# Expert stage in plain fp32 on groups of 32 array columns, raw weights in a ring of 18 pieces

## The reference

```python
logits = (t @ w_router).astype(jnp.float32)          # t: 256 x 1024
top_v, top_i = lax.top_k(logits, TOP_K)              # TOP_K = 2 of 8 experts
top_p = jax.nn.softmax(top_v, axis=-1)
combine = jnp.sum(jax.nn.one_hot(top_i, N_EXPERTS) * top_p[..., None], axis=1)
for e in range(N_EXPERTS):
    out = out + combine[:, e:e + 1] * swiglu(t, w_gate[e], w_up[e], w_down[e])
# swiglu(h, g, u, d) = (silu(h @ g) * (h @ u)) @ d; g, u: 1024 x 1408, d: 1408 x 1024
```

## Time and profile before

| | us |
|---|---|
| median of 3 runs | 1190.44 (1189.48 to 1192.33) |
| the profiled execution | 1188.07 |
| its span | 1186.0 |
| PE busy | 1136.0 (96%) |
| weight loads (PEld) busy | 1071.8 (90%) |
| DVE busy | 811.1 (68%) |
| ACT busy | 697.0 (59%) |

### The profile page before, as it was taken

How to read it: one execution, slowest core, us unless ns; L and a number is a source line. 1 busy time by engine, 2 the same in 40 slices (tenths; PEclk the granted TensorE clock), 3 DMA queues, 4 the chain that set the end, 5 groups by cost and what they waited for, 6 DMA issues and landing times.

```text
span 1186.0 us, 18538 instructions
## 1 busy us (share of the span) xinstructions
PE 1136.0 (96%) x7250; PEld 1071.8 (90%) x7250; DVE 811.1 (68%) x928; ACT 697.0 (59%) x921; POOL 15.1 (1%) x39
## 2 busy tenths in 40 slices
PE   6999999998999998999999998799999999999996
PEld 5999999998999986898999998699998989999894
DVE  5557574666455543564675475798789979878996
ACT  5635566345444433562566434777787787778775
POOL 2000000000000000000000001000000000000000
PEclk9999999998999999999999999899999999999998
DMA  7543445654665555353445566399899989999994
GB/s 234 160 149 119 142 127 153 190 168 144 176 186 178 185 186 187 107 162 128 139 134 160 144 189 236 117 336 351 304 350 343 356 298 343 343 306 347 350 347 139
DMA packets 172686, 258.25 MB, mean 218 GB/s; under 512 B 6929, under 2 KB 143185, under 8 KB 172626
## 3 DMA queue, kind: packets, MB, share of 16 engines
q1 hardware_dynamic: 172338, 256.36, 66.3%
q10 hardware_dynamic: 288, 1.05, 0.2%
HBM read 256.34 MB, written 1.05 MB: 217 GB/s over the span
## 4 chain that ended last, share of the span: by engine, by line
PE 94%; DVE 3%; ACT 1%; issue 1%; DMA 0%; DVEq 0%; SPq 0%; ACTq 0%
PE ps L1241 25%; PE ps L1242 25%; PE ps L1243 25%; PE ps L1252 7%; PE ps L1247 3%; PE ps L1249 3%; PE ps L1248 3%; PE ps L1261 1%; PE ps L1420 1%; PE ps L1591 1%; ACT xhat L609 1%; DVE hT_lo L843 1%; PE ps L1484 0%; DMA x<-in_x 0%; DVE xhat L885 0%
## 5 line engine op out<-in xcount | busy, mean ns | idle before, releaser
L837 DVE TENSOR_TENSOR w_lo<-raw,w_hi 128x1408 fp32r<-128x1408 f32 (+3 forms) x271 | 437.8, 1640 | 187.4 <-ACT w_hi L604 186.8
L604 ACT ACTIVATE w_hi<-raw 128x1408 fp32r<-128x1408 f32 (+3 forms) x271 | 371.9, 1395 | 179.9 <-DMA raw<-in_w_in 58.1
L1241 PE MATMUL ps<-w_hi,hT_hi 128*128 128x352 f32 (+6 forms) x800 | 259.7, 325 | 0.7 <-issue 0.4
L1242 PE MATMUL ps<-w_lo,hT_hi 128*128 128x352 f32 (+6 forms) x800 | 259.2, 324 | 0.0
L1243 PE MATMUL ps<-w_hi,hT_lo 128*128 128x352 f32 (+6 forms) x800 | 258.5, 323 | 0.0
L1241 PEld LDWEIGHTS ps<-w_hi,hT_hi 128*128 128x128 f32 x800 | 151.1, 189 | 3.5 <-issue 3.1
L1242 PEld LDWEIGHTS ps<-w_lo,hT_hi 128*128 128x128 f32 x800 | 151.1, 189 | 0.0
L1243 PEld LDWEIGHTS ps<-w_hi,hT_lo 128*128 128x128 f32 x800 | 151.1, 189 | 0.0
L837 DVE TENSOR_TENSOR w_lo_e<-raw_e,w_hi_e 128x1408 fp32r<-128x1408 f32 (+1 forms) x75 | 121.5, 1660 | 25.1 <-ACT w_hi_e L604 24.7
L604 ACT ACTIVATE w_hi_e<-raw_e 128x1408 fp32r<-128x1408 f32 (+1 forms) x75 | 103.7, 1414 | 15.9 <-DMA raw_e<-in_moe_w_gate 12.9
L1241 PE MATMUL ps<-w_hi,xe_hi 128*128 128x352 f32 x320 | 104.0, 325 | 0.0
(11 more groups left out here) (274 smaller groups left out, 1792.7 us busy)
## 6 DMA issues: line engine op xcount, KB each, us to landing
raw<-in_moe_w_up SPq DMA_DIRECT2D x49, 704.0 KB, 6.4
raw<-in_w_in SPq DMA_DIRECT2D x40, 768.0 KB, 4.3
raw<-in_w_in SPq DMA_DIRECT2D x32, 772.0 KB, 4.3
raw_e<-in_moe_w_gate SPq DMA_DIRECT2D x34, 704.0 KB, 6.3
raw<-in_moe_w_gate SPq DMA_DIRECT2D x32, 704.0 KB, 5.1
raw_e<-in_moe_w_down SPq DMA_DIRECT2D x24, 768.0 KB, 6.4
raw<-in_moe_w_down SPq DMA_DIRECT2D x24, 768.0 KB, 6.2
raw_e<-in_moe_w_up SPq DMA_DIRECT2D x17, 704.0 KB, 6.7
```

Of the source, the lines that this page charges most:

```text
L604: act.activation(slot(n, "hi", k), slot(n, "raw", k), ACT.Copy).then_inc(hi_done, 1)
L837: dve.tensor_tensor(slot(n, "lo", k), slot(n, "raw", k), slot(n, "hi", k).bitcast(F32), ALU.subtract).then_inc(lo_done, 1)
L1241: pe.matmul(out, hi, wh, start=first, stop=False, skip_group_check=True)
L1242: pe.matmul(out, hi, wl, start=False, stop=False, skip_group_check=True)
```

## The change

The expert stage no longer splits weights or hidden values. Gate, up and down are plain fp32 matmuls whose stationary operand is a block of 32 slots; four such blocks stand side by side in the array's four groups of 32 columns (`quads`). A pass still takes two experts, now with 64 slots each in the quads (2 x 32 + 2 x 32) and 32 further slots (`OV`) of the first, "heavy" one, whose matmuls also are spread over the four column groups. Experts 0 and 1 are the first pair; the other six are ranked by count and paired, one of the three fullest with one of the three others. Tokens beyond 96 or 64 go to listed extra passes. Weights stay raw in 18 slots (`E_RING`) of up to 768 KB, 54 pieces per pass, freed in groups of four (`e_used`). Seven pieces are issued after the V3 step, nine after `y_ready`, two after the router matmul. The slots lie over mixer buffers and over `hT`. POOL's gain product is now made in `xhat` itself, after the transposes that read it. The static part is as before, save that it no longer splits expert pieces near its end.

```diff
+HEAVY, LIGHT = 96, 64
+OV = HEAVY - LIGHT
+SLOTS = HEAVY + LIGHT
+WANT = (0, 5, 1, 4, 2, 3)
+HID = ((0, (384, 384)), (768, (384, 256)))
+SLAB = 384
+KQ = KD // 2
+for _c0, _ws in HID:
+    for _q in range(KQ):
+        E_UNITS += [(which, e, 2 * _q, 2, _c0, sum(_ws)) for which in ("gate", "up") for e in range(2)]
+for _k in range(FET):
+    E_UNITS += [("down", e, _k, 1, 0, D) for e in range(2)]
+E_RING = 18
+E_EARLY, E_MIX = 7, 16
+E_GROUP = [u // 4 for u in range(len(E_UNITS))]
...
@@ sync
             sp.wait_ge(aux_done, FIRST[1, ("V3", 0)][2] + 2)
+            for u in range(E_EARLY):
+                expert_load(u, (0, 1))
+            sp.wait_ge(y_ready, 24)
+            for u in range(E_EARLY, E_MIX):
+                expert_load(u, (0, 1))
+            sp.wait_ge(aux_done, ROUTER_AUX + 1)
+            for u in range(E_MIX, E_RING):
+                expert_load(u, (0, 1))
+            for u in range(E_RING, len(E_UNITS)):
+                sp.wait_ge(e_used, E_GROUP[u - E_RING] + 1)
+                expert_load(u, (0, 1))
...
-            for j in range(E_LEAD):
-                load(UNITS0 + j, *expert_unit(j, 0), i=iters)
@@ gpsimd
+            pool.wait_ge(w_used, UNITS0)
+            pool.memset(one[:, :, :], 0.0)
...
+            pool.wait_ge(aux_done, FIRST[LAYERS - 1, ("norm2", 0)][2] + 4)
             for tt in range(TT):
-                pool.tensor_tensor(h_rows[:, tt, :], xhat[:, tt, :], g_row[:, :], ALU.mult).then_inc(h_ready, 1)
+                pool.tensor_tensor(xhat[:, tt, :], xhat[:, tt, :], g_row[:, :], ALU.mult).then_inc(h_ready, 1)
@@ vector
+            select(lambda tt: eslot[:, tt, 0:1], lambda tt: eslot[:, tt, 1:2])
             h_rest(1)
+            link(dve.scalar_tensor_tensor(out=key, in0=cnt, scalar=float(NE), in1=iota[:, 0:NE], op0=ALU.mult, op1=ALU.subtract))
...
+            dve.tensor_copy(ids[:, POSITIONS:POSITIONS + 1], passes).then_inc(iters_ready, 1)
...
+            link(dve.tensor_reduce(pcomb[:, :, NE:POSITIONS], xs[:, :, :, :], AX.X, ALU.add))
+            for n in range(3):
+                dve.memset(pslot[:, 2 + n:3 + n], 0.0).then_inc(y_split, 1)
+            for n in range(2):
+                dve.memset(pslot[:, 5 + n:6 + n], 0.0).then_inc(turn1_read, 1)
@@ tensor
+            def quads(bank, w, lhsT, rhs, first, last):
                 for g in range(4):
+                    ins = plain(ps[g * OV:(g + 1) * OV, bank, 0:w], lhsT[:, g * OV:(g + 1) * OV], rhs[g // 2], first, last)
+                return ins
+            def hidden(half, q, i):
...
+                for s, w in enumerate(widths):
...
+                    for kind in range(2):
+                        if s == 0:
+                            for e in range(2):
+                                expert_ready(u + 2 * kind + e, i)
+                        for kk, k in enumerate(ks):
+                            ins = quads(2 * s + kind, w, xe[:, k, 0:P], [units[2 * kind + e][:, kk, cols] for e in range(2)],
+                                        k == 0, k == KD - 1)
...
+                for kk, k in enumerate(ks):
+                    for s in (1, 0):
+                        for kind in range(2):
+                            g, w = 2 * kind + s, widths[s]
+                            ins = plain(ps[g * OV:(g + 1) * OV, 4, 0:w], xe[:, k, P:SLOTS],
+                                        units[2 * kind][:, kk, s * SLAB:s * SLAB + w], k == 0, k == KD - 1)
+                ins.then_inc(e_used, 1)
...
+            with pe.Fori(0, iters) as i:
+                pe.wait_ge(xe_ready, i * 3 + 3)
+                pe.wait_ge(turn1_read, i * 2 + 2)
+                hidden(0, 0, i)
+                pe.wait_ge(y_split, i * 3 + 3)
+                for g in range(3):
+                    scatter(g)
+                hidden(0, 1, i)
+                pe.wait_ge(added, i * 4 + 1)
+                scatter(3)
+                hidden(0, 2, i)
+                hidden(0, 3, i)
+                hidden(1, 0, i)
+                turn0(i)
+                hidden(1, 1, i)
+                hidden(1, 2, i)
+                hidden(1, 3, i)
+                pe.wait_ge(turn0_read, i * 3 + 3)
+                down(0, i)
+                turn1(i)
+                down(1, i)
+                pe.wait_ge(sel_ready, i + 2)
+                gather(i + 1)
+                down(2, i)
+                pe.wait_ge(turn1_read, i * 2 + 4)
+                down(3, i)
+                down(4, i)
+                down(5, i)
```

More of the change, by code:

```diff
@@ L226 @@
             LAST_UNIT[FIRST[_l, _s][1] + _n] = _end
[L227 to L237, removed]
 def build(nc, t):
@@ L1127, in select @@
                 ins.then_inc(sel_ready, 1)
-            select((slice(0, 1), slice(1, 2)))
+            select(lambda tt: eslot[:, tt, 0:1], lambda tt: eslot[:, tt, 1:2])
             h_rest(1)
+            key, rank, extra, over, total, listed = (one[:, n, :] for n in range(6))
+            six = NE - 2
+            link(dve.scalar_tensor_tensor(out=key, in0=cnt, scalar=float(NE), in1=iota[:, 0:NE], op0=ALU.mult, op1=ALU.subtract))
+            link(dve.tensor_tensor(cmp[:, :, :], key[:, 2:NE].unsqueeze(1).broadcast_to([P, six, six]),
+                                   key[:, 2:NE].unsqueeze(2).broadcast_to([P, six, six]), ALU.is_gt))
@@ new lines, in _ @@
+            link(dve.tensor_reduce(rank[:, 2:NE].unsqueeze(2), cmp[:, :, :], AX.X, ALU.add))
+            heavy = one[:, 6, :]
+            link(dve.tensor_scalar(heavy, rank, 2.5, float(OV), ALU.is_lt, ALU.mult))
+            link(dve.memset(heavy[:, 1:2], 0.0))
+            link(dve.tensor_tensor(extra, cnt, heavy, ALU.subtract))
+            link(dve.tensor_scalar(over, extra, float(LIGHT), None, ALU.is_gt))
+            for m in (2, 3):
+                link(dve.scalar_tensor_tensor(out=over, in0=extra, scalar=float(m * LIGHT), in1=over, op0=ALU.is_gt, op1=ALU.add))
@@ new lines, in _ @@
+            for src, dst, shift in ((over, total, 1), (total, listed, 2), (listed, total, 4)):
+                dve.tensor_copy(dst[:, 0:shift], src[:, 0:shift])
+                link(dve.tensor_tensor(dst[:, shift:NE], src[:, shift:NE], src[:, 0:NE - shift], ALU.add))
+            passes = ids_f[:, POSITIONS:POSITIONS + 1]
+            last = total[:, NE - 1:NE]
+            link(dve.tensor_scalar(passes, last, 0.0, float(NE // 2), ALU.is_gt, ALU.add))
+            for m in (2, 4, 6):
+                link(dve.scalar_tensor_tensor(out=passes, in0=last, scalar=float(m), in1=passes, op0=ALU.is_gt, op1=ALU.add))
@@ L1545, in scatter, with gather @@
[L1545 to L1552 removed]
+            def gather(i):
+                for g in range(3):
+                    for k in range(3 * g, min(3 * g + 3, KD)):
+                        out = ps[:, 2 + g, (k - 3 * g) * SLOTS:(k - 3 * g + 1) * SLOTS]
+                        for n, (rows, tt) in enumerate(((h_hi, 0), (h_hi, 1), (h_lo, 0), (h_lo, 1))):
+                            ins = plain(out, rows[:, tt, k * P:(k + 1) * P], sel[:, tt, 0:SLOTS], start=n == 0, stop=n == 3)
+                    ins.then_inc(xe_filled, 1)
@@ L1554, in _ @@
             pe.wait_ge(sel_ready, 1)
             pe.wait_ge(h_hi_ready, TT)
-            gather(GATHER_AUX, h_hi)
             pe.wait_ge(h_lo_ready, TT)
-            gather(GATHER_AUX + 4, h_lo)
-            for g in range(8):
-                aux_read(pe, GATHER_AUX + g)
+            gather(0)
             pe.wait_ge(moe_zero, 1)
-            pe.wait_ge(route_ready, 1)
-            iters = pe.value_load(ids[0:1, 7:8], min_val=NE // 2, max_val=MAXPASS // 2)
+            pe.wait_ge(iters_ready, 1)
```

617 lines of the change are left out of this document (299 added, 318 removed).

## The result

| | before | after |
|---|---|---|
| median, us | 1190.41 (4 runs, 1189.48 to 1192.33) | 1134.92 (4 runs, 1134.00 to 1137.79) |
| ratio | | 0.954, 95% interval 0.9526 to 0.9553 |
| profiled execution, its span | 1188.07, 1186.0 | 1135.48, 1133.5 |
| PE busy | 96% | 95% |
| DVE, ACT busy | 811, 697 | 499, 404 |

A forecast was written before the change was run, and what follows sets the result against it. PE bounded the expert stage, DMA close behind. PE: 761.0 + 1.7 + 338.8 = 1101.5; DMA 1101.7; with 1.5 for equal limits 1103, plus 14.1 gives span 1117, plus 2.1 gives 1119 us; range 1105 to 1165.

The forecast's parts named there:

- first expert matmul: Start of the expert stage: forecast at 761.0, against 757.53 before, 3.5 us lost.
- a pass without gap: One pass of two experts on PE: 84.7 us, 338.8 for four, against 414.9 before.
- allowance for two equal limits: End of the stage: 1.5 us added because PE (1101.5) and DMA (1101.7) were expected to end together.
- behind the last expert matmul: From the last expert matmul to the span's end: 14.1 us, against 13.7 before, with a scatter of 16 matmuls.
- rival A: Expert stage: DMA alone sets the pace at 327 to 345 GB/s, time 1169 to 1149 us; chance 0.17.
- rival C: Expert stage: PE cannot be fed 860 plain records per pass at 81 ns; at 109 ns 1201 us; chance 0.10.
- PE per pass: Expert pass: 73.0 us of matmul columns plus gather, scatter, turn0 and turn1 and shape changes, 84.7 us in all.
- The way into the loop: Ahead of the stage: VectorE's small operations and memsets delay the start 3.5 us; half clock there costs 1.7 us.
- DMA: Expert weights: 124.5 MB from 769.2 on at 378 GB/s, ends 327 and 394; would end the stage at 1101.7.
- rival D: Expert loop: a fifth pass is needed, 92 us more, 1211 us; chance 0.02 with the like.
- Rival B: Expert stage: gaps put PE at 1.2 GHz for a fifth of 339 us, 34 us more, 1153 us; chance 0.09.
- What would show it: Profile signs, such as PE near 100% busy in the loop, DMA at 365 to 390 GB/s, last expert matmul 1100 to 1106.

The follow-up runs named there:

- Experiment 6: TensorE's passes written out, scatter's 128-row matmuls first, against the kernel before: 1119.30 us; with the five memsets also moved ahead of VectorE's chain, 1116.51 us.
- experiment 4: The changed kernel without the quads of four of eight gate and up blocks and seven of eleven down blocks, all transfers kept: 1097.05 us in one execution.
- experiment 8: Changed kernel with loop, new scatter order, early memsets, and 64-column matmuls in down(5) only: 1128.73 us; in down(3) to down(5): 1132.08 us.
- experiment 3: The changed kernel with the five memsets TensorE waits for moved ahead of VectorE's chain of small operations: 1133.27 us, ratio 0.953 to the kernel before.
- both small edits: Scatter's 128-row matmuls first, and five memsets moved ahead of VectorE's chain: alone on the changed kernel 1137.19 and 1133.27 us, both with passes written out 1116.51.
- experiment 2: The changed kernel with scatter's 128-row matmuls of the first three groups issued before the 64-row ones: 1137.19 us, ratio 0.9555 to the kernel before.
- experiment 1: The changed kernel with TensorE's pass code written out four times instead of looping: 1125.22 us, ratio 0.9455 to the kernel before; second time 1125.31.

## Why the prediction was right, and what it missed

Direction and range were right, the point was 16.5 us of span too low (1117 against 1133.5). By the terms of the sum:

| term | forecast | measured |
|---|---|---|
| first expert matmul | 761.0 | 761.24 |
| a pass without gap | 84.7 | 85.64 |
| jump of the loop, with the half clock behind it | not in the sum | 12.7 in the profiled execution, 9.7 in the medians |
| allowance for two equal limits | 1.5 | 0 |
| behind the last expert matmul | 14.1 | 15.2 |

The differences are 0.2 + 4 x 0.94 + 12.7 - 1.5 + 1.1 = 16.3 of the 16.5 us. That the range held has luck in it: its upper end, 1165, was set for a slow DMA, rival A, and what used that room was a cost that stands in no term and no rival.

- **The step that failed** is the sum for PE, where a pass follows the pass before it at no cost: the runs show 12.7 us of the stage, a jump of 5.9 us in each of three passes, beside which code was brought again. The trace before gave no warning: with 598 records a pass the jump took 0.22 us and was covered by matmuls. But the sum itself held the number that makes the difference, 860 plain records per pass and 937 in all, against the 598 of before (2392 in four passes). I used it for rival C (the feeding of single records) and not for the loop. A forecast that lets the code of a loop grow by half should have had that as an unknown with two ends.
- **PE per pass** was right to 1.1%. The rate of a round, taken from step V, holds over 340 us: rounds of four records of 384 columns come every 323 ns, 0.84 ns per column for the four together. At 0.84 instead of 0.85 the columns of a pass cost 0.7 us less than forecast. The gather costs 0.11 per matmul once the clock is full. The term mis-sized is scatter: 16 at 0.234, where the alternation of 128 and 64 rows makes it 0.33, 1.6 us per pass. Experiment 6 took 1.24 us of that back, a part of it by matmuls side by side. I had counted a change of shape at 0.1 us between 32 and 128 columns and not seen that scatter changes shape at every second matmul, too.
- **The way into the loop** came out as worked out: the last memset of the chain is at 760.86, TensorE waits for it 3.26 us. One thing was missed without effect: the gather ran at half clock as a whole, 7.0 instead of 3.8 us, beside the same chain. With the early memsets this hidden gather became the limit, which is why the wait there fell to 0.5 to 0.8 us and not to nothing.
- **DMA** was mis-sized the other way: 378 GB/s taken, 327 and 394 as ends, 409 to 417 measured where it was the limit (experiment 4). By the formula it would have ended about 1070 and not 1098.6, as experiment 4 shows. The forecast took both limits as equal at 1101; in truth there were some 30 us between them. The direction of my argument (larger packets are faster) agrees with these rates, though no run changes the size of the packets alone; the ends should not have been taken from packets of half the size.
- **Rival A** (DMA sets the pace) and **rival D** (a fifth pass) did not occur. **Rival B** (clock) occurred on a small scale, as a consequence of the gaps: 0.54 and 0.58 for 3.5 us behind two of them, some 3.4 us of time where the rival had 34. Its argument that only gaps of about 4 us bring half clock does not hold: here it followed two gaps of 3.0 us, and in experiment 8 one of 1.9 (0.50 for 3.4 us from 848.6), while in experiment 3 it followed none of three. **Rival C** (TensorE cannot be fed) is refuted: in rounds of 384 columns a record comes every 81 ns on the mean, over the whole stage. Something of its kind was there, though: the sequencer did fall behind, but at the jump.
- **What would show it**: "PE busy in the loop near 100%" was wrong at three places only, and there neither DMA nor VectorE was waited for. The sign for B, a window with a clock below 0.95, came without its price.

## What to carry to other kernels

Count the instructions of a loop's body on each engine when a change makes them more, and look at the jump's own row in the trace: here 0.22 us at 598 matmul records and 5.9 us at 897 and more, of which matmuls already queued covered 3.3 to 4.4. Read the instruction queue beside it: packets of code that keep coming in later passes are the sign of a body that is brought anew each time. Group TensorE's matmuls by the shape of their stationary block; each change cost 0.1 to 0.2 us, which made 64 columns worse than 32 and an alternating scatter 40% dearer. A small gain that a profile shows may not show in the time alone; combined with the edit that removed the larger waits, both small edits did.

## What the runs showed of the hardware that was not expected

- The jump with two prices, and the code packets that go with the higher one, as above.
- Two 64-row matmuls on different halves of the rows start within 7 ns of each other when nothing stands between them (experiment 2).
- Four plain fp32 matmuls on four groups of 32 columns, or two on groups of 64, run side by side: 384 columns every 323 ns, 0.84 ns per column for all of them together, over hundreds of microseconds.
- DMA of weight pieces moved 409 to 417 GB/s for 290 us (experiment 4), where the windows of before had peaked at 394.
- TensorE's clock behind the stage fell in some executions and not in others. Windows of 2.5 us in the last scatter, after (full clock, nine matmuls) and in experiment 1 (half clock, five):

```profile
1120.80:1123.30 2.50, 2.50 (x9) 1.04 (x9) 1.38 (x2) 0.72 (x2) 0.00 (x0) 1.00 0.00 0
```

```profile
1111.70:1114.20 2.50, 2.50 (x5) 1.20 (x5) 0.89 (x2) 0.72 (x2) 0.00 (x0) 0.50 0.00 0
```

  The time behind the last expert matmul is 15.2 us in the first case and 17.4 to 18.4 in the versions of the second kind. That is enough to have hidden the gain of experiment 2. It may also be much of the spread of a few microseconds within a version; with one profile of each, this is not shown.
